# Neighbourhood attention items of two grid rows and four heads, scored in quarter products, with the bias loaded per item

## The chip, the cores and the metric

The kernel runs on one core of one Trainium2 chip. The metric is the device time of one execution in microseconds (us); the lower the better. The core has TensorE (PE: matmuls, whose weight loads are listed as PEld), VectorE (DVE), ScalarE (ACT), GpSimd (POOL) and the queue engine SyncE (SP), which issues most of the DMAs. Each engine runs its own instructions in order and waits for the others by semaphores.

## The reference, cut to what matters

Three transformer-like blocks over 1024 tokens of width 1024. The change touches only the first block's neighbourhood attention: 8 heads of 64 on a grid of 16 rows by 64 columns. A query of row r attends to 8 rows of keys, and there to 16 columns around its own; the kernel computes all 64 columns and masks the rest.

```python
def one_row(r):
    r0 = jnp.clip(r - kr // 2, 0, rows - kr)          # kr = 8, rows = 16
    k_band = lax.dynamic_slice_in_dim(kg, r0, kr, axis=1)[:, :, key_cols]
    v_band = lax.dynamic_slice_in_dim(vg, r0, kr, axis=1)[:, :, key_cols]
    q_row = lax.dynamic_index_in_dim(qg, r, axis=1, keepdims=False)
    s = jnp.einsum('bjqhd,brjkhd->bhjqrk', q_row, k_band).astype(jnp.float32) * scale
    dr = r0 + jnp.arange(kr) - r + NA_WIN_R - 1
    bias = jnp.take(rpb_cols, dr, axis=1)
    s = s + jnp.transpose(bias, (0, 2, 3, 1, 4))[None]
    s = jnp.where(mask, s, -jnp.inf)
    p = jax.nn.softmax(s.reshape(s.shape[:4] + (kr * NA_KSPAN_C,)), axis=-1).reshape(s.shape)
    o = jnp.einsum('bhjqrk,brjkhd->bjqhd', p.astype(v.dtype), v_band)
# afterwards: o_na = rms_norm(o_na, na_norm_g) per head, then the output projection
```

Beside it in the same block runs the gated delta rule (GDN): 4 heads of 128, two directions, 8 chunks of 128 tokens each, a chunk's result entering the next through a state S.

## The kernel before

The kernel is one hand-ordered program. The stage of interest ("the mixers") runs GDN and the neighbourhood attention at the same time. `gdn_slots()` gives 14 slots per chunk n; in each slot every engine first does its GDN piece, then its attention piece (`na_pe`, `na_act`, `na_dve`), then the piece of the GDN output norm (`gout_*`). A slot is no barrier: an engine goes on as far as its semaphores allow, but always in this order.

GDN per chunk: slot 0 puts out the previous chunk (`step_out`, state update), slots 1 to 12 build an inverse in six levels, each a ping-pong. PE multiplies ("Q", line 1334), DVE masks into `g_gu` (1512), PE multiplies again ("X", 1334), DVE subtracts into `g_Dc` (1521) and turns it into `g_D` (1500, 1503). Slot 13 is the V product (1323) and the next chunk's keys by keys (1267).

The attention walks over 16 items k, one grid row with all 8 heads each, seven slots apart. Its parts p of an item: p 0 to 3, one score product each (line 1622) for a pair of heads, and on DVE `biased` (1740) adds the bias and takes the row maximum in one instruction; p 4 and 5, ACT takes the exponential (1684), PE turns the result (1630), ACT copies it out (1692); p 7 and 8, PE weighs the values (1648); p 9 and 10, sum of squares and scaling `n_z` (1712 to 1771); p 11, PE multiplies `n_z` by a folded identity (1676) and ACT copies to the output (1729).

A score product is a full 128 by 128 array: the 64 dimensions of two heads on the contraction side, and as weights `n_zq`, which holds head 0's queries in its upper left quarter and head 1's in its lower right one, zeros elsewhere. The result is [2 heads x 64 queries, 512 keys], one PSUM bank. All operands are f32, for which the trace shows two passes per matmul. The bias of all shifts stays in SBUF as `n_bias`, [128, 4 x 15 x 64]. A grid row whose band of keys begins at an odd row (4 of 16) has a key order in two pieces, 448 and 64 columns.

PSUM has 8 banks: each GDN direction d has three, `gbank(d, i)` = 3d + i, and the attention has banks 6 and 7: scores and turned tiles in both, its outputs in 7.

## Time and profile before

| | us |
|---|---|
| median of 3 runs | 3765.86 (3764.18 to 3771.94) |
| the profiled execution | 3769.14 |
| its span from first to last instruction | 3767.4 |
| stage of the mixers in it, first score to last finish | 379.2 to 743.2 |
| PE, DVE, ACT, POOL busy over the span | 3702.6, 2153.1, 1580.1, 80.8 |

The mean granted clock is 0.996 of full speed. The busy time of an engine says how long it had an instruction in flight, not that it set the time; matmuls overlap, so their busy times and the durations of single ones are longer than their pitch. What a step costs PE in a stream is read from one start to the next. "Idle before" is the time the engine stood before a group, with what ended it.

### The profile page before, as it was taken

The page shows a single profiled execution, that of the slowest core. Times are in us where ns is not written, and L with a number is a line of the kernel's source. Part 1 is how long each engine was busy: PE and PEld are TensorE (multiplying, and loading weights), DVE is VectorE, ACT ScalarE, POOL GpSimd, SP SyncE. Part 2 cuts the span into 40 slices and gives each one's busy share as a digit, 9 for nine tenths or more (in the row PEclk, how much of TensorE's full clock was granted, in tenths as well). Part 3 has the DMA queues.
Part 4 walks back from the last instruction along what each step waited for, and adds up shares of the span by engine and source line. Part 5 has one row for each costly group of instructions (what it writes and reads, how often), then busy time and mean ns, then how long its engine had stood idle before and what let it go on. Part 6 is the DMA issues. An engine that isn't in the chain of part 4 may idle for free.

```text
span 3767.4 us, 50718 instructions
## 1 busy us (share of the span) xinstructions
PE 3702.6 (98%) x21185; PEld 2983.0 (79%) x21185; DVE 2153.1 (57%) x3300; ACT 1580.1 (42%) x2544; POOL 80.8 (2%) x85
## 2 busy tenths in 40 slices
PE   8999898899999999999999999999999999999998
PEld 5888677778888878888788889888787778788887
DVE  5641767776334668757588655266555266555333
ACT  5452566534333544435353442333433233434333
POOL 0000121000000000000000000000000000000000
PEclk9999999999999999999999999999999999999999
DMA  5122101233422222222222322222222222223222
GB/s 196 46 73 64 31 19 38 86 103 97 116 95 95 91 88 73 95 91 94 90 79 84 100 92 90 88 86 79 84 95 91 94 84 84 79 95 118 95 92 87
DMA packets 116363, 327.83 MB, mean 87 GB/s; under 512 B 27288, under 2 KB 34472, under 8 KB 116136
## 3 DMA queue, kind: packets, MB, share of 16 engines
q1 hardware_dynamic: 113896, 319.07, 25.6%
q0 software_dynamic: 2240, 5.51, 0.7%
q8 instruction: 169, 2.77, 0.3%
q14 instruction: 58, 0.48, 0.0%
HBM read 307.99 MB, written 18.09 MB: 87 GB/s over the span
## 4 chain that ended last, share of the span: by engine, by line
PE 95%; DVE 2%; ACT 1%; issue 1%; DMA 0%; SPq 0%; ACTq 0%; DVEq 0%
PE ps L329 54%; PE ps L307 28%; PE ps L1622 2%; PE ps L1323 2%; PE ps L807 1%; PE ps L1648 1%; PE ps L2785 1%; PE ps L1031 1%; PE ps L1334 1%; PE ps L1630 0%; DVE n_s L1740 0%; ACT n_s L1684 0%; PE ps L2220 0%; PE ps L2247 0%; PE ps L1364 0%
## 5 line engine op out<-in xcount | busy, mean ns | idle before, releaser
L329 PE MATMUL ps<-a,w_hi 128*128 128x512 f32 (+1 forms) x6064 | 1838.2, 388 | 3.8 <-issue 2.1
L329 PEld LDWEIGHTS ps<-a,w_hi 128*128 128x128 f32 x6064 | 1110.1, 188 | 262.0 <-issue 12.0
L329 PE MATMUL ps<-a,w_lo 128*128 128x512 f32 (+1 forms) x3032 | 1147.3, 385 | 0.0
L268 DVE TENSOR_TENSOR w_lo<-w_raw,w_hi 128x1024 fp32r<-128x1024 f32 x539 | 658.0, 1221 | 396.6 <-ACT w_hi L263 393.8
L263 ACT ACTIVATE w_hi<-w_raw 128x1024 fp32r<-128x1024 f32 x539 | 563.5, 1050 | 517.0 <-DMA w_raw<-in_w_mlp 323.8
L329 PEld LDWEIGHTS ps<-a,w_lo 128*128 128x128 f32 x3032 | 562.5, 188 | 119.7
L307 PE MATMUL ps<-h_hi,w_hi 128*128 128x512 f32 x1528 | 485.4, 399 | 0.0
L307 PE MATMUL ps<-h_hi,w_lo 128*128 128x512 f32 x1528 | 479.1, 395 | 0.0
L307 PE MATMUL ps<-h_lo,w_hi 128*128 128x512 f32 x1528 | 478.8, 395 | 0.0
L374 DVE TENSOR_TENSOR h_lo<-u_sq,h_hi 128x512 fp32r<-128x512 f32 x192 | 132.9, 692 | 461.5 <-ACT h_hi L364 460.7
L390 DVE TENSOR_TENSOR xT<-xT,ps 128x1024 f32<-128x1024 f32 x191 | 232.9, 1220 | 247.3 <-PE ps L307 246.4
L307 PEld LDWEIGHTS ps<-h_hi,w_lo 128*128 128x128 f32 x1528 | 288.1, 189 | 65.8
L307 PEld LDWEIGHTS ps<-h_lo,w_hi 128*128 128x128 f32 x1528 | 288.1, 189 | 65.5
L307 PEld LDWEIGHTS ps<-h_hi,w_hi 128*128 128x128 f32 x1528 | 284.9, 189 | 69.0 <-issue 4.4
L359 ACT ACTIVATE u_act<-ps 128x512 f32<-128x512 f32 x128 | 76.6, 598 | 346.2 <-PE ps L329 346.1
L2191 DVE SCALAR_TENSOR_TENSOR mixh<-c_pad,params,mixh 128x512 f32<-128x512 f32 x240 | 163.7, 744 | 0.0
L363 ACT ACTIVATE u_sq<-u_act 128x512 f32<-128x512 f32 x192 | 121.3, 632 | 18.3 <-ACT u_act L359 1.1
L359 ACT ACTIVATE u_act<-ps,params 128x512 f32<-128x512 f32 x64 | 44.1, 688 | 197.4 <-PE ps L329 197.4
L364 ACT ACTIVATE h_hi<-u_act 128x512 fp32r<-128x512 f32 x192 | 118.1, 615 | 0.0
L396 DVE TENSOR_TENSOR xT<-xT,ps 128x512 f32<-128x512 f32 x48 | 32.9, 686 | 133.9 <-PE ps L329 133.9
L2847 ACT ACTIVATE l_e<-l_e 128x256 f32<-128x256 f32 x56 | 23.4, 418 | 140.8 <-DVE l_e L2883 139.8
L1622 PE MATMUL ps<-n_k,n_zq 128*128 128x512 f32 (+2 forms) x160 | 73.9, 563 | 6.9 <-DVE n_small L1740 6.9
(394 smaller groups left out, 2971.8 us busy)
## 6 DMA issues: line engine op xcount, KB each, us to landing
...
w_raw<-in_w_in SPq DMA_DIRECT2D x107, 512.0 KB, 3.4
...
```

The costliest lines, as they stand in the source:

```text
L263: nc.scalar.activation(w_hi[u.z][:, :], w_raw[u.z][:, :], ACT.Copy).then_inc(w_hi_done[u.z], 1)
L268: nc.vector.tensor_tensor(w_lo[u.z][:, :], w_raw[u.z][:, :], w_hi[u.z][:, :].bitcast(F32), ALU.subtract).then_inc(w_split[u.z], 1)
L307: last = nc.tensor.matmul(ps[:, u.bank + c, :], w[:, k * 256 + c * P:k * 256 + (c + 1) * P], act[:, (u.first + k) % RING, :], start=(k == ...
L329: last = nc.tensor.matmul(ps[:, bank, 0:t1 - t0], w[:, k * P:(k + 1) * P], a[:, h, low, k, t0:t1], start=(i_k == 0 and i == 0), stop=(i_k ...
L359: nc.scalar.activation(u_act[:, s, :], ps[:, u.bank, :], ACT.Relu, bias=bias).then_inc(bank_free(u), 1)
L363: nc.scalar.activation(u_sq[:, s, :], u_act[:, s, :], ACT.Square)
L364: nc.scalar.activation(h_hi[:, u.chunk % RING, :], u_act[:, s, :], ACT.Square).then_inc(hid_hi, 1)
L374: nc.vector.tensor_tensor(h_lo[:, r, :], u_sq[:, u.chunk % 2, :], h_hi[:, r, :].bitcast(F32), ALU.subtract)\
L390: nc.vector.tensor_tensor(two, two, ps[:, u.bank:u.bank + 2, :], ALU.add).then_inc(bank_free(u), 1)
L1323: last = nc.tensor.matmul(pbank(b)[:, h, :], lhsT[:, h, :], rhs[:, h, :], start=start, stop=stop)
L1622: last = nc.tensor.matmul(ps[:, score_bank(k, c), t0:t1], n_zq[k % 2][:, c, :], n_k[:, c, row * GRID:row * GRID + t1 - t0], start=True, st ...
L2191: nc.vector.scalar_tensor_tensor(y, x, w, y, op0=ALU.mult, op1=ALU.add).then_inc(c_tap, 1)
```

## The change

An item is now one chunk of two grid rows (2c and 2c+1) with four of the eight heads; there are still 16 items. `item(k)` gives the chunk and the first pair of heads. A score call covers one pair of heads and both rows: four matmuls of 64 by 64 weights, one in each quarter of the array (contraction side: the head i; output side: the row j), which write the halves of banks 6 and 7. So the calls stand at p 0 and p 2 in place of p 0, 1, 2, 3. The queries `n_q` are loaded as they are, without zeros, with one DMA in place of two.

The bias differs between the two rows, so its slice per item is gathered: the masked table (now `n_tab`) is stored once to memory (`na_tab`), and `bias_item_sp` loads [128, 4, 512], 1 MB, into one of two buffers `n_bias`, whenever the slice differs from that two items before (10 items of 16). `biased` is then always one instruction of 512 columns; the second maximum of the odd rows is gone.

The attention's outputs go to bank 1 (even k) or 4 (odd k), which GDN also uses: so Q moves to bank 2 or 5, where X is, V to bank 0 or 3, and there are new waits: the GDN's output product of direction 1 and its k by q product wait for `n_z`, `weigh` waits for GDN's readers. The finish is two 128 by 128 transposes in place of eight 64 by 64 products; it waits for the next item's `biased`, since its bank 7 holds scores.

Cut diff (Q's, V's and the ACT and DVE lines that only follow the new banks and the renamed tiles are left out):

```diff
@@ -741,8 +741,9 @@
         g_bytok = xs.take("g_bytok", [2 * TC * GH, P])
         xs2 = Region(x_at, x_at + 4 * DC * T)
         n_k = xs2.take("n_k", [P, NP, T])
-        n_bias = xs2.take("n_bias", [P, NP, 2 * KR - 1, GRID])
-        n_mask = xs2.take("n_mask", [P, GRID])
+        n_tab = Region(xs2.at, xs2.stop).take("n_tab", [P, NP, 2 * KR - 1, GRID])
+        n_bias = [xs2.take(f"n_bias{i}", [P, NP, BAND]) for i in range(2)]
+        n_mask = main_tail.take("n_mask", [P, GRID])
 
         G_LOG, G_CUM, G_TOT, G_BETA, G_NEGDEC, G_KDEC, G_LAST, G_TMP = range(8)
         G_CUMB, G_NCUM = G_TOT, G_TMP
...
@@ -1356,6 +1357,9 @@
             def step_out(m, d):
                 pe.wait_ge(gs["vn"], last_once(m, d))
                 pe.wait_ge(gs["qd"], once(m, d))
+                pe.wait_ge(gs["qk"], once(m, d))
+                if d:
+                    pe.wait_ge(na["z"], 2 * m + 2)
                 for h in range(GH):
                     o = pbank(gbank(d, 1))[:, h, :]
 
...
@@ -1407,6 +1407,10 @@
                 if s == 8 and n >= 0:
                     for d in range(2):
                         c = toks(chunk_of(n, d))
+                        if n:
+                            pe.wait_ge(gs["oe"], once(m, d))
+                        if d == 0:
+                            pe.wait_ge(na["z"], 2 * n + 1)
                         heads(gbank(d, 1), g_kT[:, :, c], g_qT[:, :, c]).then_inc(gs["kq"], 1)
                 if s == 10 and n >= 0:
                     for d in range(2):
...
@@ -1591,36 +1598,51 @@
         def na_rows(i):
             return [(k, i - ROW_STEPS * k) for k in (i // ROW_STEPS - 1, i // ROW_STEPS) if 0 <= k < ROWS and i - ROW_STEPS * k <= 11]
 
-        def spans(k):
-
-            r0 = BANDS[k]
-            dr0 = r0 - RO[k] + KR - 1
+        def item(k):
+
+            return CHUNKS[k // 2], 2 * (k % 2)
+
+        def spans(r):
+
+            r0 = band(r)
+            dr0 = r0 - r + KR - 1
             if r0 % 2 == 0:
                 return [(0, BAND, r0, dr0)]
             return [(GRID, BAND, r0, dr0), (0, GRID, r0 + KR - 1, dr0 + KR - 1)]
 
-        def score_bank(k, c):
-
-            return 6 if k else 6 + c % 2
-
-        def out_heads():
-            return ps[:, 7, 0:NP * GRID].rearrange("p (c x) -> p c x", c=NP)
+        def item_bias(k):
+
+            return [(j, t0, t1, dr) for j in range(2) for t0, t1, _, dr in spans(2 * item(k)[0] + j)]
+
+        def new_bias(k):
+            return k < 2 or item_bias(k) != item_bias(k - 2)
+
+        def bias_loads(k):
+
+            return sum(2 * len(item_bias(i)) for i in range(k % 2, k + 1, 2) if new_bias(i))
+
+        def out_heads(k):
+            return ps[:, gbank(k % 2, 1), 0:NP * GRID].rearrange("p (t x) -> p t x", t=NP)
 
         def na_pe(pe):
-            def score(k, c):
-                if c == 0 and k:
-                    pe.wait_ge(na["ptc"], NP * k - 1)
-                if c == 0:
-                    pe.wait_ge(zq_in[k % 2], X_IN + 32 * (k // 2) + 32)
-                if k == 0 and c < 2:
-                    pe.wait_ge(nv_act, NV_LAST.index(6 + c) + 1)
-                elif k == 0:
-                    pe.wait_ge(na["m"], c - 1)
-                elif c:
-                    pe.wait_ge(na["m"], NP * k + c)
-                for t0, t1, row, _ in spans(k):
-                    last = nc.tensor.matmul(ps[:, score_bank(k, c), t0:t1], n_zq[k % 2][:, c, :], n_k[:, c, row * GRID:row * GRID + t1 - t0], start=True, stop=True)
-                last.then_inc(na["s"], 1)
+            def score(k, pair):
+                c, first = item(k)
+                if pair == 0:
+                    pe.wait_ge(zq_in[k % 2], X_IN + 16 * (k // 2) + 16)
+                    if k:
+                        pe.wait_ge(na["ptc"], NP * k)
+                    else:
+                        pe.wait_ge(nv_act, TC)
+                else:
+                    pe.wait_ge(na["m"], NP * k + 2)
+                pieces = [(j, t0, t1, row) for j in range(2) for t0, t1, row, _ in spans(2 * c + j)]
+                for j, t0, t1, row in pieces:
+                    for i in range(2):
+                        part = slice(GRID * i, GRID * i + GRID)
+                        last = nc.tensor.matmul(ps[GRID * j:GRID * j + GRID, 6 + i, t0:t1], n_q[k % 2][part, pair, GRID * j:GRID * j + GRID],
+                                                n_k[part, first + pair, row * GRID:row * GRID + t1 - t0], start=True, stop=True)
+                        if (j, t0, t1, row) == pieces[-1]:
+                            last.then_inc(na["s"], 1)
 
             def turn(k, c):
                 pe.wait_ge(na["p"], NP * k + c + 1)
@@ -1630,30 +1652,33 @@
                     last = nc.tensor.transpose(ps[:, 6 + c % 2, t * P:(t + 1) * P], n_s[:, c, t * P:(t + 1) * P], const("ident"))
                 last.then_inc(na["pt"], 1)
 
-            def weigh(k, c):
-                r0 = BANDS[k]
+            def weigh(k, t):
+                c, first = item(k)
+                head = (first + t // 2) * P + t % 2 * GRID
                 pe.wait_ge(na["ptc"], NP * k + NP)
-                for t in range(KR // 2):
-                    if r0 % 2 == 0:
-                        v = n_v[:, r0 // 2 + t, c * P:(c + 1) * P]
-                    elif t == 0:
-                        i = ODD.index(k)
-                        pe.wait_ge(vx_in[i % 2], X_IN + 32 * (i // 2) + 32)
-                        v = n_vx[i % 2][:, c * P:(c + 1) * P]
-                    else:
-                        v = n_v[:, (r0 + 1) // 2 + t - 1, c * P:(c + 1) * P]
-
+                if k % 2:
+                    pe.wait_ge(gs["qk"], once(k // 2, 1))
+                elif k:
+                    pe.wait_ge(gs["oe"], once(k // 2 - 1, 0))
+                for b in range(KR // 2):
                     for j in range(2):
+                        r0 = band(2 * c + j)
+                        if r0 % 2 == 0:
+                            v = n_v[:, r0 // 2 + b, head:head + GRID]
+                        elif b == 0:
+                            i = ODD.index(k // 2)
+                            pe.wait_ge(vx_in[i % 2], X_IN + 32 * (i // 2) + 32)
+                            v = n_vx[i % 2][:, head:head + GRID]
+                        else:
+                            v = n_v[:, (r0 + 1) // 2 + b - 1, head:head + GRID]
                         part = slice(GRID * j, GRID * j + GRID)
-                        last = nc.tensor.matmul(ps[part, 7, c * GRID:(c + 1) * GRID], n_pt[c][:, t, part], v[:, part], start=(t == 0),
-                                                stop=(t == KR // 2 - 1))
+                        last = nc.tensor.matmul(out_heads(k)[part, t, :], n_pt[t][:, b, part], v, start=(b == 0), stop=(b == KR // 2 - 1))
                 last.then_inc(na["av"], 1)
 
-            pe.wait_ge(nb_done, 1)
             for i in range(GDN_STEPS):
                 for k, p in na_rows(i):
-                    if p < 4:
-                        score(k, p)
+                    if p in (0, 2):
+                        score(k, p // 2)
                     if p == 5:
                         normed = i - EARLY + 6 - OUT_FIRST - 8
                         if normed >= 0:
@@ -1670,11 +1695,11 @@
                         weigh(k, 2 * (p - 7) + 1)
                     if p == 11:
                         pe.wait_ge(na["z"], k + 1)
-                        for c in range(NP):
-                            for j in range(2):
-                                part = slice(GRID * j, GRID * j + GRID)
-                                last = nc.tensor.matmul(ps[part, 7, c * GRID:(c + 1) * GRID], n_z[part, c, :], const("fold")[part, :],
-                                                        start=True, stop=True)
+                        if k + 1 < ROWS:
+                            pe.wait_ge(na["m"], NP * (k + 1) + NP)
+                        for i in range(2):
+                            last = nc.tensor.transpose(ps[:, 7, i * P:(i + 1) * P], n_z[:, 2 * i:2 * i + 2, :].rearrange("p t x -> p (t x)"),
+                                                       const("ident"))
                         last.then_inc(na["f"], 1)
                 yield
...
         def na_dve(dve):
-            def biased(k, c):
-                dve.wait_ge(na["s"], NP * k + c + 1)
+            def biased(k, t):
+                dve.wait_ge(na["s"], NP * k + t + 1)
+                if t == 0:
+                    dve.wait_ge(bias_in[k % 2], 16 * bias_loads(k))
                 if k:
-                    dve.wait_ge(na["pt"], NP * (k - 1) + c + 1)
-                for j, (t0, t1, _, dr) in enumerate(spans(k)):
-                    bias = n_bias[:, c, dr:dr + (t1 - t0) // GRID, :].rearrange("p r x -> p (r x)")
-                    ins = nc.vector.tensor_tensor_reduce(n_s[:, c, t0:t1], ps[:, score_bank(k, c), t0:t1], bias, 1.0, -3.0e38, op0=ALU.add, op1=ALU.max,
-                                                         accum_out=n_small[:, N_MAX + j, c:c + 1])
-                ins.then_inc(na["m"], 1)
+                    dve.wait_ge(na["pt"], NP * (k - 1) + t + 1)
+                nc.vector.tensor_tensor_reduce(n_s[:, t, :], ps[:, 6 + t % 2, :], n_bias[k % 2][:, t, :], 1.0, -3.0e38, op0=ALU.add, op1=ALU.max,
+                                               accum_out=n_small[:, N_MAX, t:t + 1]).then_inc(na["m"], 1)
...
         def queries_sp(sp, k):
+            c, first = item(k)
             if k >= 2:
                 sp.wait_ge(na["s"], NP * (k - 1))
-            for j in range(2):
-                part = slice(GRID * j, GRID * j + GRID)
-                sp.dma_start(n_zq[k % 2][part, :, part], g["nq1"][:, part, GRID * RO[k]:GRID * RO[k] + GRID].rearrange("c p t -> p c t"))\
-                    .then_inc(zq_in[k % 2], 16)
+            sp.dma_start(n_q[k % 2][:, :, :], g["nq1"][first:first + 2, :, toks(c)].rearrange("c p t -> p c t")).then_inc(zq_in[k % 2], 16)
+
+        def bias_item_sp(sp, k):
+            c, first = item(k)
+            if k >= 2:
+                sp.wait_ge(na["m"], NP * (k - 1))
+            for j, t0, t1, dr in item_bias(k):
+                for i in range(2):
+                    src = g["na_tab"][GRID * i:GRID * i + GRID, first:first + 2, dr:dr + (t1 - t0) // GRID, :].rearrange("p c r x -> p c (r x)")
+                    sp.dma_start(n_bias[k % 2][GRID * j:GRID * j + GRID, i:NP:2, t0:t1], src).then_inc(bias_in[k % 2], 16)
...
         def mixers_sp(sp):
-            sp.wait_ge(n_zero, 1)
+            sp.wait_ge(stored, 16 * 2 * GH)
             queries_sp(sp, 0)
             queries_sp(sp, 1)
+            sp.wait_ge(nb_done, 1)
+            sp.dma_start(g["na_tab"], n_tab[:, :, :, :]).then_inc(stored, 16)
+            sp.wait_ge(stored, 16 * 2 * GH + 16)
+            bias_item_sp(sp, 0)
+            bias_item_sp(sp, 1)
             sp.wait_ge(nv_act, TC)
             odd_v_sp(sp, 0)
             odd_v_sp(sp, 1)
```

The order on PE in the middle of the fourth chunk (slots 3 to 6): the two weigh calls, the score calls and between them Q and X, of which each is sixteen small matmuls. Before, one 128-row score after every step:

```order
L1648 MATMUL ps<-n_v,n_pt_135 64x64 x8
L1622 MATMUL ps<-n_k,n_zq_83 128x512
L1334 MATMUL ps<-g_gu_108,g_D_110 64x8x4
...
L1648 MATMUL ps<-n_v,n_pt_137 64x64 x8
L1622 MATMUL ps<-n_k,n_zq_83 128x512
L1334 MATMUL ps<-g_Dc_112,g_A_114 64x4x8
...
L1622 MATMUL ps<-n_k,n_zq_83 128x512
L1334 MATMUL ps<-g_gu_108,g_D_110 64x4x8
```

Now, in the same stretch:

```order
L1675 MATMUL ps<-n_v,n_pt_137 64x64 x8
L1642 MATMUL ps<-n_k,n_q_83 64x512 x4
L1335 MATMUL ps<-g_gu_110,g_D_112 64x8x4
...
L1675 MATMUL ps<-n_v,n_pt_139 64x64 x8
L1335 MATMUL ps<-g_Dc_114,g_A_116 64x4x8
...
L1642 MATMUL ps<-n_k,n_q_83 64x512 x4
L1335 MATMUL ps<-g_gu_110,g_D_112 64x4x8
```

Four full products per item have become two groups of four quarter products; the one between the second weigh pair and Q is gone, and the one behind the next X too.

The order on SP ahead of the mixers and in the first chunk. Before, queries (`n_zq`), shifted values (`n_vx`) and decay rows (`g_row`):

```order
L1956 DMA n_zq_82<-nq 64x4x64 x2
L1956 DMA n_zq_83<-nq 64x4x64 x2
L1965 DMA n_vx_139<-n_v 64x512 x2
L1965 DMA n_vx_140<-n_v 64x512 x2
L1925 DMA g_row_141<-gate_rows 128x512
```

Now:

```order
L1971 DMA n_q_82<-nq 128x2x128
L1971 DMA n_q_83<-nq 128x2x128
L1995 DMA na_tab<-n_tab 128x3840
L1980 DMA n_bias_106<-na_tab 64x2x512 x4
L1980 DMA n_bias_107<-na_tab 64x2x512 x4
L1988 DMA n_vx_141<-n_v 64x512 x2
L1988 DMA n_vx_142<-n_v 64x512 x2
L1945 DMA g_row_143<-gate_rows 128x512
```

The store of the table and eight loads of it stand ahead of the values and the decay rows.

## Rows read from the trace of the kernel before

**Rows 1.** Page, part 1: busy time, share of the span, instructions of each engine.
```profile
PE 3702.6 (98%) x21185; PEld 2983.0 (79%) x21185; DVE 2153.1 (57%) x3300; ACT 1580.1 (42%) x2544; POOL 80.8 (2%) x85
```

**Rows 2.** Windows, one per chunk: length, busy us per engine, clock, DMA.
```profile
423.00:466.00 43.00, 39.51 (x683) 31.54 (x682) 32.75 (x105) 28.17 (x83) 7.43 (x6) 1.00 0.09 26
510.50:555.00 44.50, 40.99 (x682) 32.32 (x681) 30.95 (x100) 26.27 (x77) 7.43 (x6) 0.96 0.07 20
648.00:698.00 50.00, 44.24 (x687) 35.30 (x686) 35.21 (x111) 28.93 (x81) 7.87 (x6) 0.93 0.10 27
```

**Rows 3.** Chain of waits, 381 to 743 us, shares by line.
```profile
by line: PE ps L1622 16.5%; PE ps L1323 16.4%; PE ps L1648 10.3%; PE ps L1334 6.9%; issue 5.1%; PE ps L1630 4.9%; DVE n_s L1740 4.9%; ACT n_s L1684 4.9%; PE ps L1364 3.9%; PE ps L1363 3.5%; PE ps L1267 3.5%; DVE g_D L1503 2.9%; PE ps L1353
```

**Rows 4.** Line 1622, the scores: ns min/median/max, forms, who waits.
```profile
L1622 PE MATMUL ps<-n_k,n_zq x160: 219/592/1220, 379.2 to 719.4; 128*128 128x512 f32 x96, 128*128 128x448 f32 x32, 128*128 128x64 f32 x32
...
  DVE n_small L1740: 17.8, 49
...
  DVE n_s L1740: 53.7, 40
```

**Rows 5.** Timeline of PE from 519.3 us: start, us, what, [idle before].
```profile
520.35 1.15 PE L1648 MATMUL ps<-n_v,n_pt 128*64 128x64 f32 x32
521.43 1.13 PE L1622 MATMUL ps<-n_k,n_zq 128*128 128x512 f32 x2
522.49 0.67 PE L1334 MATMUL ps<-g_gu,g_D 64*64 64x32 f32 x32
523.09 1.15 PE L1648 MATMUL ps<-n_v,n_pt 128*64 128x64 f32 x32
```

**Rows 6.** Timeline of PE, 544 to 546 us.
```profile
544.04 0.68 PE L1346 MATMUL ps<-g_Dc,g_A 64*64 64x64 f32 x16
544.65 1.15 PE L1648 MATMUL ps<-n_v,n_pt 128*64 128x64 f32 x32
```

**Rows 7.** Timeline of PE, 1443.2 to 1446 us (block 2 scores).
```profile
1443.38 2.00 PE L2247 MATMUL ps<-s_k,s_q 64*128 64x256 f32 x16
1445.31 0.72 PE L329 MATMUL ps<-a,w_hi 128*128 128x512 f32 x2
```

**Rows 8.** Line 1740, biased: ns min/median/max, forms.
```profile
L1740 DVE CUSTOM_DVE_ANT_0 n_s<-ps,n_bias x80: 219/682/693, 381.1 to 720.3; 128x512 f32<-128x512 f32 x48, 128x448 f32<-128x448 f32 x16, 128x64 f32<-128x64 f32 x16
```

**Rows 9.** Timeline of DVE, 515 to 532 us.
```profile
522.60 0.69 DVE L1740 CUSTOM_DVE_ANT_0 n_s<-ps,n_bias 128x512 f32<-128x512 f32 x1 [1.29 <-PE ps L1622]
...
525.33 0.69 DVE L1740 CUSTOM_DVE_ANT_0 n_s<-ps,n_bias 128x512 f32<-128x512 f32 x1 [0.61 <-PE ps L1622]
...
527.35 0.49 DVE L1512 TENSOR_TENSOR g_gu<-ps,g_lev 128x128 f32<-128x128 f32 x2
...
531.25 0.69 DVE L1740 CUSTOM_DVE_ANT_0 n_s<-ps,n_bias 128x512 f32<-128x512 f32 x1 [1.24 <-PE ps L1622]
```

**Rows 10.** Timeline of PE, 525 to 533 us.
```profile
528.09 0.67 PE L1334 MATMUL ps<-g_gu,g_D 64*64 64x32 f32 x32 [0.88 <-DVE g_gu L1512]
529.14 2.07 PE L1622 MATMUL ps<-n_k,n_zq 128*128 128x512 f32 x2 [0.38 <-DVE n_small L1740]
```

**Rows 11.** Timeline of ACT, 543.9 to 549.9 us.
```profile
547.06 2.45 ACT L1299 ACTIVATE g_dec<-g_dec,g_gates 128x128 f32<-128x128 f32 x8
549.42 0.36 ACT L1712 ACTIVATE n_zsq<-ps 128x256 f32<-128x256 f32 x1
```

**Rows 12.** Queries' DMAs on SP, line 1956: ns min/median/max, first and last start.
```profile
L1956 SPq DMA_DIRECT2D n_zq<-nq x32: 573/610/1513, 332.0 to 671.6; - x32
```

**Rows 13.** DMA, 299 to 316 us: issues, KB each, us to landing.
```profile
n_bias<-rpb_rows SPq DMA_DIRECT2D x8, 240.0 KB, 5.7
```

**Rows 14.** Windows: around a fall of the clock, and ahead of the stage.
```profile
525.70:529.10 3.40, 1.99 (x49) 0.97 (x42) 3.29 (x13) 0.50 (x2) 0.00 (x0) 1.00 0.00 0
529.10:532.50 3.40, 3.36 (x10) 2.33 (x10) 2.09 (x8) 0.00 (x0) 0.00 (x0) 0.50 0.02 5
346.00:379.00 33.00, 33.00 (x153) 27.02 (x152) 4.32 (x10) 4.80 (x9) 0.00 (x0) 1.00 0.00 0
```

71 lines of the change are left out of this document (31 added, 40 removed).

## Prediction

> **What bounds the kernel now.** I read the page first, then the windows by chunk, the chain of waits, the score line and the timelines of one chunk. PE is busy 98% of the span [rows 1], but the stage of the mixers (379 to 743 us) is looser: a chunk takes 43.0 us with PE busy 39.51, DVE 32.75 and ACT 28.17, a later one 44.5, and those in which the GDN output norm joins 50.0 [rows 2]. So PE is nearly the bound, with a small idle part in which DVE and ACT set the pace. In the chain of waits over the stage the score line 1622 is the largest piece, 16.5% of 362 us, which is 60 us [rows 3]; nearly every score product lies on the path. Around them DVE waits 53.7 us in total for scores, and PE 17.8 us for DVE's reading of the last one [rows 4].
>
> **The change part by part.**
>
> *The scores on PE, removed.* 16 items times 4 products. A product is two passes and takes 521.43 to 522.49 = 1.06 us [rows 5]. That is 64 x 1.06 = 67.8 us (the 16 in two pieces, 448 and 64 columns, taken as the same).
>
> *The scores on PE, added.* 16 items times 2 groups of four quarter products, each of two passes of 512 columns. Nothing in the trace has four quarters with 512 columns; three rows bound it. Four quarters at once: Q and X are 16 quarter products of 32 columns, 32 passes in 522.49 to 523.09 = 0.60 us, 19 ns each [rows 5]. Line 1346 uses two quarters at a time: 16 passes in 544.04 to 544.65 = 0.61 us, 38 ns each [rows 6]. Twice the quarters, half the time per pass: four quarters do work side by side, at least where loading weights is what takes the time. Two halves of the contraction side with a longer stream: 16 passes of 256 columns in 1443.38 to 1445.31 = 1.93 us, so 0.24 us per pair of passes [rows 7], while 512 columns on the whole array take 0.53 a pass: the two halves overlap fully. Line 1648, two halves of the output side, takes 32 passes in 1.08 us, 34 ns each, less than the 38 of the quarters. So I take a group as two passes of 512 columns, twice 0.24 to 0.48 for twice the columns each: 0.9 us plus the start, 0.93. The bounds: 0.93 if all four overlap; 1.8 if two at a time do; about 3.7 if none does. I take 0.93, since all rows with less than the whole array show overlap. Sum 32 x 0.93 = 29.8 us; the eight odd items add two short pieces per group, about 0.12 us each, 2 us. PE loses 67.8 - 31.8 = 36 us of work.
>
> By the Trainium skill, TensorEngine Tiling (Array Packing), section Restrictions and Gotchas, different row tiles cannot use one PSUM bank at the same time. In Q and X both row halves write into one bank, and they take 19 ns a pass all the same [rows 5], so the trace doesn't bear it out as a serialization; here the two heads write banks 6 and 7 anyway. Were the rule to bite somewhere, the result would be the second rival's.
>
> *The finish.* Eight quarter products with 16 passes, at 38 ns [rows 6] 0.6 us, become two transposes with 4 passes; a 128-column pass is about a quarter of the 0.53 of a 512-column one, so 0.13, 0.5 in all. 0.1 x 16 = 1.6 us at most; I count it in the chunk below.
>
> *DVE.* The four odd rows lose 16 extra instructions of 64 columns, at 0.22 us (the least of the line) to 0.69 [rows 8], and four small ones: 4 to 10 us over the stage, none in the early chunks, and half of it in cover. Its four waits on scores per item become one: after the first `biased` of a pair, the second finds its bank full.
>
> *The walk through one chunk.* The fourth chunk runs from 504.02 to 548.62, 44.6 us. At 521.43 the first score starts on both kernels. Before, DVE runs `biased` at 522.60 after 1.29 us of idling and the second at 525.33 after 0.61 [rows 9]; that one holds up its turns and `g_gu` at 527.35, and so PE, which waits 0.88 for X at 528.09 [rows 9, 10]. After, the second `biased` runs without a wait, and X comes at about 527.3, 0.8 earlier: less than the 2.1 us of scores cut on PE, since DVE is now the slower one. Then the 2.07 us of the last score goes (at half clock, [rows 10]) and with it DVE's wait of 1.24 [rows 9]; DVE's own work (scaling, turns, `g_gu`) puts the next X at 531.9 in place of 534.8, 2.9 earlier. Behind slot 8 the same pattern comes again for the next item, with two products of 1.06 ahead of the V product: about 4.6 earlier there. At the chunk's end ACT's exponentials (2.45) stand ahead of the squares at 549.42 [rows 11], and DVE's chain behind the squares takes a us of the gain away and gives it back as PE no longer puts a score between keys by keys and `step_out`. I get 39 to 39.5 us for the chunk at full clock, and allow 0.7 for the clock (below) and the new waits: 40.0, a gain of 4.6. PE then has 41.0 - 8.5 + 3.7 - 0.2 = 36.0 us of work in 40.0 [rows 2], DVE 31: tight but possible.
>
> *New waits.* `step_out` of direction 1 waits for `n_z` of the odd item, behind it the state update, the finish and the next Q. In the walk both come within 0.4 us of each other; it can cost 0 to 0.5 a chunk, and it is in the 0.7. The k by q product waits for `n_z` of slot 6, two slots past. The finish waits for the next item's last `biased`, which has no wait of its own any more. V in bank 0 or 3 waits for `kd`, three slots past. These cost nothing in that walk, and up to 0.3 each if DVE slips.
>
> *The table.* Storing 1.97 MB and loading two items of 1 MB go behind the masked table and to where the first load of queries stands, 332.0 [rows 12]. Eight DMAs of 240 KB landed at 5.7 us each, all between 300 and 316 [rows 13]: 1.9 MB in some 15 us. So the store ends by 347 and the loads by 363; from 346 to 379 the DMA engines are empty, [rows 14], and the first `biased` is at 381. Cover: 17 us. Later loads are 1 MB, some 8 us, issued about 20 us ahead of use on an SP queue that otherwise waits. Nothing on the path. The first score waits for the last copy of the values, about 0.8 us later, and gives it back but for 0.2.
>
> *The sum.* Chunk 0: 4.0; chunks 1 to 3: 3 x 4.6 = 13.8; chunks 4 to 6, longer by pieces of the output norm that ACT and DVE pace: 3 x 4.0 = 12.0; chunk 7, with only one item to score: 2.3; less 0.2 at the start. 31.9 us. What follows the stage is PE-bound and moves as a whole. The profiled execution was 3769.1 us, so 3737; against the median, 3765.9 - 32 = 3734.
>
> **The clock.** Right before a fall the engine was busy 1.99 of 3.40 us; then it had the lower of its two levels, 1.2 in place of 2.4 GHz, for 3.4 us [rows 14]. The mean clock is 0.96 in most chunks, one such fall each, 0.93 in a later one [rows 2]. The change thins out PE's work exactly there (slots 5 and 6), so falls will not get rarer. By the Trainium skill, TensorE: Matmul & The Clock Gate, section on the two states, the engine runs at half rate unless kept busy, which is what the row shows; it speaks against a change that takes PE's densest work away.
>
> **The rivals.**
> *Half the gain is eaten by DVE and ACT* (0.12): PE falls idle and the ping-pong sets the chunk. For it: the first X gains only 0.8 of 2.1. Against it: DVE is busy 31 of 44.5. If the gain per chunk is 2.3: 18 us, 3748.
> *Quarters overlap only in pairs at 512 columns* (0.09): a group takes 1.8; PE saves 67.8 - 57.6 - 2 = 8 us, with the finish 10: 3756. For it: the passes of 32 columns are so short that weight loading may hide it [rows 5]. Against it: the two contraction halves overlap in full at 256 columns [rows 7], and nothing shows all four.
> *The clock, slower than before* (0.05): a chunk has 34.5 us of PE work at full clock (39.5 - 8.5 + 3.7 - 0.2) and some 3.5 of idling. With a share f of the time at half clock it is 34.5 / (1 - f/2) + 3.5; it passes 44.6 once f is over 0.32, against 0.08 now. At f = 0.5 a chunk takes 49.5, 5 more, +35 us: 3800.
> *It does not do what it says* (0.04): the bias arrives late or a new wait holds each chunk for 4 us, so that the gain is gone: 3762 to 3770.
> The forecast has 0.70.
>
> **How the numbers follow.** Faster (by over 0.2%, 7.5 us, about what a measurement of this kernel can tell from none): 0.70 + 0.12 + 0.09 = 0.91. Same 0.03, slower 0.06, from the last two. The range: low end, all of PE's saving plus four us of half-clock scores, 3766 - 44 = 3722; high end, the pairwise rival, 3757.
>
> **What would show it.** Right: a score group of 8 passes that takes about 0.93 us up to the next start; the score line under 8% of the stage's chain; DVE's waits for scores under 25 us; chunks of 39 to 41 us; PE waiting on `g_gu` more than before; n_bias loads with no one waiting. Wrong: groups of 1.8 us; a PEclk under 0.85 in the chunks; PE waiting for `n_z` ahead of `step_out` by over 1 us; the stage starting later than 380 us.

## The result, and the profile after

The changed kernel takes 3742.36 us (median of four runs, 3740.22 to 3745.01). The kernel before took 3766.53 beside it (3764.18 to 3771.94). The ratio is 0.9934, with a 95% interval of 0.9917 to 0.9951, so 24 us are gained where 32 were forecast; 3742 lies inside the range of 3722 to 3757. The profiled execution spans 3740.3 us in place of 3767.4, at a mean clock of 0.994.

In the lines of the changed kernel 1622 has become 1642 (scores), 1740 is 1764 (bias and maximum), 1648 is 1675 (value products), 1630 is 1652 (turns), 1334 is 1335 (Q and X), 1323 is 1324, 1684 is 1709 (exponents), 1692 is 1717 (turned copies).

The page after, against [rows 1], busy time of each engine:

```profile
PE 3668.1 (98%) x21121; PEld 2968.0 (79%) x21121; DVE 2148.3 (57%) x3262; ACT 1580.2 (42%) x2544; POOL 81.5 (2%) x85
```

PE lost 34.5 us of busy time; 36 were forecast, and up to 1.6 for the finish. DVE lost 4.8, where 4 to 10 were forecast.

Windows of three chunks, against [rows 2] (length, busy us of PE, PEld, DVE, ACT, POOL, clock, DMA):

```profile
497.40:537.00 39.60, 34.93 (x680) 29.69 (x676) 30.66 (x99) 26.48 (x77) 7.45 (x6) 1.00 0.32 76
578.40:620.90 42.50, 37.32 (x690) 31.38 (x686) 32.00 (x102) 28.04 (x80) 7.46 (x6) 0.96 0.16 46
666.20:709.60 43.40, 36.26 (x670) 31.15 (x665) 32.14 (x101) 29.68 (x82) 2.51 (x2) 0.96 0.11 30
```

A chunk with the clock full throughout takes 39.6 us, PE busy 34.9 in it and DVE 30.7.

The score group on PE, against [rows 5]:

```profile
512.73 1.15 PE L1675 MATMUL ps<-n_v,n_pt 128*64 128x64 f32 x32
513.81 1.09 PE L1642 MATMUL ps<-n_k,n_q 64*64 64x512 f32 x8
514.72 0.62 PE L1335 MATMUL ps<-g_gu,g_D 64*64 64x32 f32 x32
```

From 513.81 to 514.72 are 0.91 us for four quarter products of 512 columns, less than one product of the whole array took before (1.06). The four overlap in full. The groups of the items with an odd band, 12 passes with the short pieces among them, take the same 0.91 (the 0.12 that I added for them does not appear):

```profile
532.66 1.10 PE L1642 MATMUL ps<-n_k,n_q 64*64 64x512 f32 x12
533.57 0.63 PE L1347 MATMUL ps<-g_Dc,g_A 64*64 64x64 f32 x16
```

The chain of waits over 378 to 720 us, against [rows 3]:

```profile
by line: PE ps L1324 13.3%; issue 8.4%; PE ps L1675 7.7%; PE ps L1642 7.0%; DVE n_s L1764 5.8%; PE ps L1335 5.7%; DVE g_D L1508 5.2%; ACT n_s L1709 3.9%; PE ps L1652 3.6%; PE ps L1367 3.5%; DVE g_gu L1517 3.2%; PE ps L1368 3.1%; PE ps L1354
```

Scores went from 16.5% of it to 7.0%, and VectorE's lines came up. What the score line waits for (`n_small`) and who waits for it (`n_s`), against [rows 4] (us, times):

```profile
L1642 PE MATMUL ps<-n_k,n_q x320: 216/589/1112, 379.7 to 689.1; 64*64 64x512 f32 x96, 64*64 64x448 f32 x32, 64*64 64x64 f32 x32
...
  DVE n_small L1764: 13.9, 16
...
  DVE n_s L1764: 32.9, 15
```

Timeline of VectorE over the same stretch as the walk's, against [rows 9]:

```profile
514.95 0.69 DVE L1764 CUSTOM_DVE_ANT_0 n_s<-ps,n_bias 128x512 f32<-128x512 f32 x1 [1.26 <-PE ps L1642]
...
517.00 0.68 DVE L1764 CUSTOM_DVE_ANT_0 n_s<-ps,n_bias 128x512 f32<-128x512 f32 x1
...
519.00 0.49 DVE L1517 TENSOR_TENSOR g_gu<-ps,g_lev 128x128 f32<-128x128 f32 x2
...
520.04 0.69 DVE L1764 CUSTOM_DVE_ANT_0 n_s<-ps,n_bias 128x512 f32<-128x512 f32 x1
```

From 514.95 VectorE has no gap until 525.7: the first bias waits 1.26 us for its scores, and all behind it goes through without a wait. The chain in this stretch, 512.7 to 523 us, is now VectorE's but for the two PE groups ahead of it:

```profile
by line: DVE n_s L1764 23.9%; DVE g_D L1508 12.8%; PE ps L1675 11.2%; PE ps L1642 10.6%; issue 10.5%; DVE g_S L1535 8.3%; DVE g_D L1505 7.7%; DVE g_Dc L1526 6.3%; DVE g_gu L1517 4.7%; DVE n_small L1781 3.3%; DVE n_small L1764 1.1%; DVE n_sm
```

Before, the same stretch (520.35 to 530.6 us of the kernel before) was PE's:

```profile
by line: PE ps L1622 41.0%; PE ps L1648 21.8%; DVE n_s L1740 13.5%; DVE g_D L1503 8.6%; PE ps L1334 5.8%; DVE g_gu L1512 4.8%; DVE g_D L1500 3.5%; DVE n_small L1761 3.3%; issue 2.9%; DVE n_small L1759 0.7%; DVE n_small L1763 0.3%; DVE n_sma
```

The bias is loaded from the table with nobody waiting, at a median of 4.7 us for each of 36 loads (against [rows 13]):

```profile
n_bias<-na_tab SPq DMA_DIRECT2D x36, 256.0 KB, 4.7
```

The stage measured by the start of each V product (`g_R` by `g_Dt`), which ends a chunk:

| | V of chunk 0 | steps to the V of chunks 1 to 7 | last finish |
|---|---|---|---|
| before | 418.2 | 41.2, 44.6, 44.6, 44.9, 47.5, 50.9, 45.0 | 742.9 |
| after | 418.6 | 38.9, 39.9, 39.6, 41.4, 42.5, 45.3, 43.4 | 717.3 |
| gain | -0.4 | 2.3, 4.7, 5.0, 3.5, 5.0, 5.6, 1.6 | 25.6 in all |

Between the last V and the last finish 1.7 us are lost again. So the early and last pieces fall short, the middle ones are as forecast. Of the 0.4 us lost up to the V of chunk 0, 0.5 lie ahead of the first score (379.69 for 379.20); from there the chunk takes 38.95 us, before 39.02. At the start the changed kernel runs with a low clock. PE, and the window behind it:

```profile
379.69 1.09 PE L1642 MATMUL ps<-n_k,n_q 64*64 64x512 f32 x8 [0.78 <-ACT n_v L826]
382.19 1.09 PE L1642 MATMUL ps<-n_k,n_q 64*64 64x512 f32 x8 [1.41 <-DVE n_small L1764]
...
385.75 1.97 PE L1652 MATMUL ps<-consts,n_s 128*128 128x128 f32 x8 [2.03 <-ACT n_s L1709]
```

```profile
385.00:395.00 10.00, 9.25 (x120) 7.36 (x124) 3.83 (x13) 7.30 (x20) 4.97 (x4) 0.51 0.58 146
```

Three idle stretches of 0.8, 1.4 and 2.0 us, then 10.2 us at the lower of the two levels (granted 0.51), and 6.8 more from 402 on. The kernel before idled 0.6 and 1.2 us there, and 0.7 later, and ran at full clock until 403. The trace's clock records add up to 37.4 us at the lower level in the stage, and 23.8 before.

### The profile page after: what moved, and what is told of

The parts are those of the page before. It is cut to its first block, busy times and chain, and to the rows that moved or that the text cites. A ratio compares the mean times of both kernels' runs of the same rounds, so it can differ in the third digit from the quotient of the medians.

```text
span 3740.3 us, 50657 instructions
## 1 busy us (share of the span) xinstructions
PE 3668.1 (98%) x21121; PEld 2968.0 (79%) x21121; DVE 2148.3 (57%) x3262; ACT 1580.2 (42%) x2544; POOL 81.5 (2%) x85
## 4 chain that ended last, share of the span: by engine, by line
PE 94%; DVE 3%; ACT 2%; issue 1%; DMA 0%; SPq 0%; ACTq 0%; DVEq 0%
PE ps L329 54%; PE ps L307 28%; PE ps L1324 1%; PE ps L808 1%; PE ps L2815 1%; PE ps L1032 1%; PE ps L1675 1%; PE ps L1642 1%; DVE n_s L1764 1%; PE ps L1335 1%; DVE g_D L1508 0%; PE ps L2250 0%; PE ps L2277 0%; ACT n_s L1709 0%; PE ps L2239 0%
## 5 line engine op out<-in xcount | busy, mean ns | idle before, releaser
L329 PEld LDWEIGHTS ps<-a,w_hi 128*128 128x128 f32 x6064 | 1110.0, 188 | 260.5 <-issue 10.6
L363 ACT ACTIVATE u_sq<-u_act 128x512 f32<-128x512 f32 x192 | 121.3, 632 | 18.3 <-ACT u_act L359 1.1
L464 ACT ACTIVATE a<-mixh 128x512 fp32r<-128x512 f32 x64 | 40.5, 633 | 78.8 <-DVE mixh L498 77.6
```

The costliest lines, as they stand in the source:

```text
L329: last = nc.tensor.matmul(ps[:, bank, 0:t1 - t0], w[:, k * P:(k + 1) * P], a[:, h, low, k, t0:t1], start=(i_k == 0 and i == 0), stop=(i_k ...
L363: nc.scalar.activation(u_sq[:, s, :], u_act[:, s, :], ACT.Square)
L464: nc.scalar.activation(a[:, m.half, 0, c, META:W], src, ACT.Copy).then_inc(m.s["hi"], 1)
```

## The experiments

All times are medians; each kernel ran beside the kernel before, which took 3766.1 to 3768.0 us. "More" and "less" are against the 3742.36 of the changed kernel, unless another kernel is named.

### What a microsecond on each engine costs

**Every score group twice**

```diff
-                for j, t0, t1, row in pieces:
+                for again in range(2):
+                    for j, t0, t1, row in pieces:
...
-                        if (j, t0, t1, row) == pieces[-1]:
+                            if again and (j, t0, t1, row) == pieces[-1]:
```

> The changed kernel with every group of quarter products issued twice (the same result into the same banks, the second one is waited for). It adds 32 groups of 0.91 us = 29 us of PE work. Theory A (PE is still what mostly sets the chunk, and what was cut from it came back nearly whole): 22 to 29 us more than the changed kernel, about 3768. Theory B (after the change DVE and ACT set the ping-pong, and PE idles): 5 to 14 us more, about 3752. If the lower clock is what ate part of the gain, the denser PE shows fewer stretches at half clock than the 37 us of the changed kernel.

3758.26 us (3752.76 to 3762.02), ratio 0.9973 (0.9964 to 0.9982): 15.9 more, of 28.8 us that PE was given (65.3 busy on the line in place of 36.5). So 55% comes through, between the two theories (5 to 14 and 22 to 29 us). PE is no longer the full bound, but its work still counts. The stage is at the lower clock level for 27.2 us in place of 37.4, less, as expected of a denser PE.

**An additional copy on ScalarE ahead of each turned copy** (the copy is used by nothing)

```diff
+                act.wait_ge(na["ptc"], NP * k + c)
+                nc.scalar.activation(n_scr[:, :], ps[:, 6 + c % 2, :], ACT.Copy)
                 nc.scalar.activation(n_pt[c][:, :, :].rearrange("p t x -> p (t x)"), ps[:, 6 + c % 2, :], ACT.Copy).then_inc(na["ptc"], 1)
```

> The changed kernel with one more ACT copy of 512 columns (to a tile nobody reads) ahead of each of the 64 copies of turned tiles: 64 x 0.5 = 32 us of ACT work, each between the turns on PE and the weighing. Theory A (PE): under 12 us more. Theory B with ACT as the one that sets the chunk: 25 us or more. With DVE as the one: under 12 us.

```profile
L1719 ACT ACTIVATE n_scr<-ps 128x512 f32<-128x512 f32 x64 | 38.0, 594 | 12.5 <-PE ps L1653 7.1
```

3768.07 us (3765.46 to 3769.38), ratio 1.0002 (0.9993 to 1.0012): 25.7 more of 38.0 added, 68%; theory B with ScalarE had 25 or more. The lower level took 64.7 us of the stage in place of 37.4, so that a part of this is the clock's. ScalarE, busy 64% of the stage, has no room where it counts: the exponents, the turns and the turned copies follow one another.

**An additional copy on VectorE ahead of each bias**

```diff
+                if NP * k + t:
+                    dve.wait_ge(na["m"], NP * k + t)
+                nc.vector.tensor_copy(n_scr[:, :], ps[:, 6 + t % 2, :])
                 nc.vector.tensor_tensor_reduce(n_s[:, t, :], ps[:, 6 + t % 2, :], n_bias[k % 2][:, t, :], 1.0, -3.0e38, op0=ALU.add, op1=ALU.max,
```

> Ahead of each of the 64 bias-and-maximum instructions VectorE copies the same 512 scores from the bank to a scratch tile (some 0.6 us each, 38 us in all; the copy is used by nothing). Theory A (PE is the bound, VectorE and ScalarE have room between the score groups): half or less comes through, under 19 us, 3745 to 3761 us. Rival B (the first score group, the bias of tiles 0 and 1 and the second group follow one another with PE idle, and the exponents wait for the last bias): nearly all of it comes through, 30 us or more, 3772 us or above.

```profile
L1767 DVE COPY n_scr<-ps 128x512 f32<-128x512 f32 x64 | 43.7, 683 | 34.1 <-PE ps L1643 33.5
```

3778.05 us (3772.11 to 3781.16), ratio 1.0025 (1.0015 to 1.0034): 35.7 more of 43.7 added, 82%. The rival's case. Not all of it is VectorE's own: with PE waiting more, the lower clock level took 81.7 us of the stage in place of 37.4. In chunk 1, which has no such stretch, 3.8 us came of 5.5 added, 70%.

The three prices, 55, 68 and 82%, sum to far more than one: a chain goes to and fro between the engines, and each of them is on it for a part of a chunk. Their order, however, does not rank the engines, since the clock differs between the runs. Chunks with the same clock in both kernels give 67% for PE (chunk 3, no low stretch: 42.0 us for 39.6, of 3.6 added), 70% for VectorE (chunk 1 above) and 89% for ScalarE (chunk 2, 3.4 us at the lower level in each: 44.1 for 39.9, of 4.75 added), from one execution each. As an estimate, the cut at the prices of the medians, 34.5 x 0.55 + 4.8 x 0.82 = 23 us, is close to the 24 gained.

### The overlap of the quarters

**Quarter by quarter, each piece cut in two**

```diff
-                for j, t0, t1, row in pieces:
-                    for i in range(2):
+                for j in range(2):
+                    for i in range(2):
+                        for t0, t1, row, _ in spans(2 * c + j):
+                            half = (t0 + t1) // 2
+                            for u0, u1 in ((t0, half), (half, t1)):
...
```

> Each score group is issued quarter by quarter, the pieces of a quarter one behind another and each cut in two (16 products a group where there were 4 or more), so that neighbours in the queue mostly need the same quarter of the array. Theory A (the four quarters run side by side only because neighbours in the queue belong to different quarters): a group grows from 0.91 us to between 2 and 3.7 us (one quarter alone is 512 columns at two passes, some 1.1 us), PE gets 30 to 90 us more of busy time, and by the 15 to 19 us that came through of 29 in the doubled score groups the time goes to 3760 to 3790 us. Rival B (the array sorts it out, whatever the order): the group stays below 1.2 us and the time within 4 us of the changed kernel.

PE's timeline of a group of an even band and of one of an odd band:

```profile
514.62 1.11 PE L1644 MATMUL ps<-n_k,n_q 64*64 64x256 f32 x16
515.53 0.64 PE L1335 MATMUL ps<-g_gu,g_D 64*64 64x32 f32 x32
...
535.35 1.84 PE L1644 MATMUL ps<-n_k,n_q 64*64 64x256 f32 x21
537.01 0.27 PE L1347 MATMUL ps<-g_Dc,g_A 64*64 64x64 f32 x2
```

3748.65 us (3747.73 to 3750.12), ratio 0.9948 (0.9934 to 0.9963): 6.3 more. Neither theory holds as written. With four passes of a quarter in a row (even bands, 16 passes) the group still takes 0.91: the array does sort it out. In an item with an odd band one of the two rows has two pieces, so that its quarters get eight passes in a row and the other row's four (24 passes in all). This group takes 1.66 to 2.0, where the changed kernel's 12 passes over the same columns, quarter after quarter in turn, take 0.91. In the group at 535.35 the trace has the first passes of three quarters at 535.35 to 535.38 and that of the fourth, which stands in the queue behind the eight of the third, only at 536.19. Its passes are then all that is in flight:

```profile
L1644 PE MATMUL ps<-n_k,n_q 64*64 64x224 f32 x3 | 0.7, 349 | 0.0
```

(PE's lines by form, 536.7 to 537.0 us.) The number of passes alone is hardly the reason, since 32 of Q or X go in 0.60 us [rows 5]. Sixteen such groups times 0.75 or more are 12 us of PE work and 6.3 us of time, half, as in the doubled groups. So the way in which the products are written carries a part of the gain, and a group as long as the pairwise rival's 1.8 does occur, for another order and another cut. The late fourth quarter speaks for the order; no run has the order without the cut.

### The clock

**Products that nothing uses in the start's idle stretches**

```diff
                     else:
+                        pe.wait_ge(nv_act, 2)
+                        filler(256)
                         pe.wait_ge(nv_act, TC)
                 else:
+                    if k == 0:
+                        filler(512)
+                        filler(128)
                     pe.wait_ge(na["m"], NP * k + 2)
...
+                if k == 0 and c == 0:
+                    filler(512)
+                    filler(256)
+                    filler(128)
```

> The changed kernel with six products that nobody reads, put into bank 0 in the gaps where PE waits at the start of the stage (before the first score group, before the second, before the first turn; 0.5, 1.3 and 1.8 us). Theory C (the first chunk lost its gain because PE stood still 4.2 us of 6, and its clock then was at half for 10.2 and 6.8 us): the clock holds over 385 to 409 us, the first V product comes at about 414.5 in place of 418.6, and the end 4 us earlier, 3738. Rival (the start is late for the wait on the values' last copy and the ACT chain): no change in the first V product, or later by the fillers, within 1 us.

The first 26 us of the stage, with the fillers and without:

```profile
378.00:404.00 26.00, 20.57 (x396) 14.45 (x395) 17.26 (x58) 13.11 (x35) 7.48 (x6) 0.90 0.54 129
```

```profile
378.00:404.00 26.00, 18.02 (x342) 12.49 (x341) 16.73 (x56) 11.71 (x31) 7.47 (x6) 0.77 0.39 98
```

The clock is 0.90 in place of 0.77, and the V product of chunk 0 starts at 415.2 in place of 418.6. The median, 3740.63 (3737.82 to 3741.83), ratio 0.9927 (0.991 to 0.9943), is 1.7 us lower, within the intervals. Counted from the first score, chunk 0 takes 35.9 us in place of 38.95, with 6.8 us at the lower level in place of 17.0. In this execution, then, the low clock cost chunk 0 most of its gain; whether it does so in the median is taken up with the last pair.

**The same, and fillers in every chunk**

```diff
+                    if k % 2:
+                        pe.wait_ge(gs["S"], once(k // 2, 0))
+                        filler(256)
...
+                if s == 6 and n >= 0:
+                    nc.tensor.matmul(ps[:, 0, 0:256], all_ones, n_k[:, 0, 0:256], start=True, stop=True)
```

> The start's fillers as in the run before, and in each of the eight chunks two more idle stretches filled with a product of 256 columns that nothing uses: ahead of the second score group of the odd item and ahead of the third level's second products. Theory A (the half-clock stretches that remain, some 27 us of them in the stage, each begin behind an idle stretch of PE and cost about half of their length): they go for the most part, and the stage gains up to 10 us on the start's fillers alone, 3731 to 3737 us. Rival B (the fillers delay the chain by as much as the clock returns, or the falls begin elsewhere): within 3 us of the kernel with the start's fillers, 3738 to 3744 us, or above it.

3738.24 us (3735.65 to 3739.59), ratio 0.9918 (0.9902 to 0.9935): 2.4 below the run before, 20.4 us at the lower level in place of 27.2. This is the rival's case (within 3 us); another 2 us are within what the intervals leave open.

### Where the wait sits

**The second score group a slot later** (with the start's fillers, as all kernels below but the last)

```diff
-                    if p in (0, 2):
-                        score(k, p // 2)
+                    if p in (0, 3):
+                        score(k, p // 3)
...
-                    if p < 4:
+                    if p < 2:
                         biased(k, p)
+                    if p == 3:
+                        biased(k, 2)
+                        biased(k, 3)
```

> The start's fillers as before, and the second score group of each item one slot later, behind the level products of the two heads (slot 3 in place of 2, with both of its bias instructions in slot 3). Theory A (PE stands idle for the bias of tile 1 in slot 2 of each item, 7 us in the stage, and that is on the path): the stage gains 3 to 7 us, 3733 to 3738 us. Rival B (the exponents then wait, since the last bias comes later by one PE pass; ScalarE's chain from exponent to turned copy was found on the path): no gain or a loss, 3741 to 3755 us.

```profile
L1776 DVE CUSTOM_DVE_ANT_0 n_s<-ps,n_bias 128x512 f32<-128x512 f32 x64 | 42.7, 688 | 38.7 <-PE ps L1650 38.5
L1650 PE MATMUL ps<-n_k,n_q 64*64 64x512 f32 (+2 forms) x320 | 40.4, 595 | 0.4 <-ACT n_v L826 0.3
```

3758.94 us (3752.94 to 3768.02), ratio 0.9979 (0.9969 to 0.9989). PE's wait for the bias is gone to nearly nothing (0.3 us), and 18.3 us are lost against the kernel with the start's fillers, more than rival B allowed (3755). VectorE now waits 38.5 us for scores in place of 31.4, but most of the loss is the clock's: chunk 1, with the clock full, takes 39.8 us, only 0.8 more than with the fillers alone, and chunk 2, with 10.2 us at the lower level, 4.5 more:

```profile
455.40:499.50 44.10, 38.86 (x669) 32.24 (x669) 31.00 (x100) 26.48 (x77) 7.44 (x6) 0.88 0.28 68
```

68.0 us of the stage are at the lower level in place of 27.2. The work is the same (DVE 31.0, ACT 26.5 in the chunk). What has changed is that PE idles once for 2.7 us ahead of X, where it idled 0.7, 0.9 and 1.1 us apart from each other. In chunks 2 to 5 the clock fell for 10.2 us at this stretch, in chunk 1 it did not:

```profile
438.18 0.67 PE L1335 MATMUL ps<-g_gu,g_D 64*64 64x32 f32 x32 [2.67 <-DVE g_gu L1517]
...
478.81 1.08 PE L1335 MATMUL ps<-g_gu,g_D 64*64 64x32 f32 x32 [2.73 <-DVE g_gu L1517]
```

So one long idle stretch makes a fall likely, not certain. This is the mechanism of the clock rival, and its price was about right: its formula gives 4.5 us more for 10.2 us of a 44.1 us chunk at half clock; 4.5 were measured, of which some 0.8 came with full clock too.

**The value products of tiles 0 and 1 a slot later, so that the next item's first scores stand ahead of them**

```diff
-                    if p in (7, 8):
-                        weigh(k, 2 * (p - 7))
-                        weigh(k, 2 * (p - 7) + 1)
+                    if p == 8:
+                        for t in range(NP):
+                            weigh(k, t)
```

> The start's fillers as before, and the value products of an item's tiles 0 and 1 move one slot later, so that the first score group of the next item stands directly behind the level products of slot 3 or 10 and in front of the next level products. Theory A (VectorE is the engine that has no room, all that was added to it came through, and it waits 32.9 us in 15 waits for score groups that stand behind value products of 1.1 us): the waits fall by 1 us each, the steps of the chunks by 1 to 2 us each, 3724 to 3732 us. Rival B (VectorE then waits for the next thing, since the level products themselves come no earlier): within 3 us of the kernel with the start's fillers, 3738 to 3744 us.

```profile
L1776 DVE CUSTOM_DVE_ANT_0 n_s<-ps,n_bias 128x512 f32<-128x512 f32 x64 | 43.9, 688 | 16.3 <-PE ps L1650 15.8
```

3726.31 us (3724.36 to 3727.47), ratio 0.989 (0.9875 to 0.9905): 14.3 less than with the start's fillers alone, as theory A had it (3724 to 3732). VectorE's wait for scores fell from 31.4 us in that kernel to 15.8, 15.6 us, and nearly all of it came through, with no engine given less work. A part may be the clock's, since 20.4 us of the stage are at the lower level in place of 27.2. Of the single moves tried, this is the wait that pays most.

**Exponents ahead of the last output copy on ScalarE**

```diff
-                for k, p in na_rows(i):
+                for k, p in reversed(na_rows(i)):
```

> The start's fillers as before; ScalarE does the first two exponents of an item ahead of the output copy of the item before, for whose transposes it waits 1.9 and 2.8 us in a chunk. Theory A (ScalarE's chain from exponent to turned copy is on the path, as 26 us of 32 that came through there say): PE's waits for n_s and n_pt (10 us in the stage) fall by half or more and 0.5 to 1.5 us a chunk is gained, 3730 to 3737 us. Rival B (VectorE sets the pace there and PE only waits elsewhere): within 3 us of the kernel with the start's fillers, 3738 to 3744 us.

```profile
L1664 PE MATMUL ps<-consts,n_s 128*128 128x128 f32 x256 | 35.1, 280 | 3.4 <-ACT n_pt L1729 2.6 <-ACT g_vt L1839 0.4 <-ACT n_s L1721 0.3
```

3734.32 us (3733.18 to 3735.64), ratio 0.9912 (0.9897 to 0.9927): 6.3 less than with the start's fillers alone. PE's idle time ahead of the turns is 3.4 us, where it was 11.5 in that kernel (12.4 in the changed one).

**Both, and the squares a slot earlier**

```diff
-                    if p == 9:
+                    if p == 8:
                         act.wait_ge(na["av"], NP * k + NP)
```

> Both edits of the two kernels beside it and a third: the squares for the output norm one slot earlier on ScalarE, ahead of the exponents of slot 12, behind which VectorE waits 2.2 us for them in a chunk. Theory A (all three waits are on the path that runs through VectorE): 2.5 to 4 us a chunk, 3712 to 3724 us. Rival B (the waits share one cover, so that only one of them pays): no better than the better of the two kernels beside it by more than 2 us.

3723.82 us (3723.27 to 3726.13), ratio 0.9885 (0.9869 to 0.9902): 2.5 below the better of the two. The steps of chunks 1 to 4 are 37.8 to 38.1, but 14.3 + 6.3 do not add up: theory A's 3712 to 3724 is met only at its edge, and what it rests on (each wait pays for itself) is not.

**Two moves on VectorE besides**

```diff
-                if s in (2, 4) and 0 < n < TC:
-                    d = s // 2 - 1
+                if s in (1, 3) and 0 < n < TC:
+                    d = s // 2
...
-                if s == 8 and n >= 0:
+                if s == 9 and n >= 0:
                     for d in range(2):
                         dve.wait_ge(gs["kq"], once(n, d))
```

> The three edits and the start's fillers as in the run before, and on VectorE two more moves: the state updates of slots 2 and 4 stand in slots 1 and 3 behind the masked products, where VectorE waits 1.0 and 0.4 us for the level products, and the masking of g_qk stands in slot 9 in place of 8, where it waits 0.6 and 0.2 us for PE. Theory A (VectorE sets the pace of a chunk and each of its waits is on the path): up to 2 us a chunk for seven chunks, 3711 to 3720 us. Rival B (PE waits already for the masked products, and the moved work delays the level results by as much as it saves): within 3 us of the kernel with the three edits, 3721 to 3727 us.

Waits of VectorE ahead of the level results, in the kernel with three edits and with five:

```profile
L1526 DVE TENSOR_TENSOR g_Dc<-g_Dc,ps 128x128 f32<-128x128 f32 x80 | 19.2, 281 | 10.7 <-PE ps L1335 10.6
```

```profile
L1526 DVE TENSOR_TENSOR g_Dc<-g_Dc,ps 128x128 f32<-128x128 f32 x80 | 19.1, 280 | 2.7 <-PE ps L1335 2.5
```

3714.09 us (3711.93 to 3715.73), ratio 0.9862 (0.9848 to 0.9877): 9.7 less than with three edits. The waits went from 10.6 to 2.5 us and, at `g_qk`, from 8.1 to none, since work that does not need the level results now stands where VectorE waited for them; its waits for scores fell too, from 14.3 to 7.4. Of these 23 us less than half came through as time.

**The five moves without fillers**

> The five moves without the start's fillers. Theory A (the half-clock stretch at the start is the same whatever follows, and the fillers gave 1.7 us by the medians and 2.5 us by the spans): 1 to 4 us above the kernel beside it. Rival B (the fillers' gain was a draw of where the clock fell): within 1 us of it.

3711.81 us (3710.44 to 3713.46), ratio 0.9858 (0.9842 to 0.9874). It is 2.3 us faster than with the fillers, where theory A had 1 to 4 more and rival B the same within 1, so neither is met, though the spreads of the two kernels overlap. No gain of the fillers is shown. PE idles 0.78, 1.41 and 2.03 us at the start as in the changed kernel, and this time the clock fell at 384 for 6.8 us and at 401 for 3.4, in place of 10.2 and 6.8; the V product of chunk 0 starts at 414.3. From the first score it takes 35.3 us, as with the fillers (35.4), where the changed kernel took 38.95. The same idle stretches are followed by low stretches of different length. This version beats both kernels: 54.3 us less than before, 30.6 less than the changed one. A chunk at full clock:

```profile
450.70:487.30 36.60, 33.81 (x670) 28.99 (x668) 30.36 (x100) 26.31 (x78) 7.45 (x6) 1.00 0.35 81
```

PE is busy 33.8 of 36.6 us there.

## Why the prediction was right, and where it was off

*The score group.* Right: 0.91 for 0.93. (The working's own rows give twice 0.48, or 0.96; the 0.93 was rounded down on the way, 1 us over 32 groups.) The choice between the bounds of 0.93, 1.8 and 3.7 decided the forecast, and the quarter-by-quarter run shows that a group near the middle bound can be had: 1.66 to 2.0 for odd bands, at 6.3 us for half of the groups.

*The walk through a chunk.* Right: 39 to 39.5 us were forecast at full clock, 39.6 measured; 40.0 with the clock, and the steps of chunks 1 to 3 are 38.9 to 39.9. VectorE as the next bound after the first bias is what the chain shows.

*Chunk 1.* Off by the baseline. I took the 44.6 us of the third step for all three early chunks; but the first took 41.2 in the trace of before. It had no fall of the clock, which half of a 3.4 us stretch, 1.7 us, can explain; the rest stays open. The gain there was 2.3 where 4.6 were in the sum.

*Chunk 0.* The term that failed: 4.0 forecast, 0.1 measured from the first score on, and the start 0.5 late for 0.2. The walk's pattern was carried to a chunk whose start is different: PE has nothing beside the scores to do, so that shorter scores turn into idle time (0.6 and 1.2 us became 1.4 and 2.0), and 17.0 us at the lower clock level followed where 3.4 had been. From the first score on, the chunk takes 3.0 us less with fillers and 3.6 less in the last kernel's execution without them (the five moves themselves did little there: 35.4 with fillers, for 35.9). So 3 to 3.6 of the 4.0 are there when the low stretch is shorter. The forecast had said that falls would not get rarer, and put 0.7 a chunk on it, but nothing on the start. How often the long low stretch comes was not settled; two pairs of medians disagree on the fillers' sign (1.7 less, 2.3 more).

*Chunks 4 to 6 and 7.* 14.1 measured for 12.0; 1.6 for 2.3. *Behind the last V* 1.7 are lost, which the sum did not have. The largest new wait there is the one on `n_z` ahead of `step_out`:

```profile
713.59 0.46 PE L1367 MATMUL ps<-g_qd,g_S 128*128 128x128 f32 x2 [1.99 <-DVE n_z L1791]
```

I had named it at 0 to 0.5 a chunk. In `step_out` it takes 3.5 us in four waits in the stage and 2.0 of them here, where no other work of PE stands between. That it accounts for the 1.7 is read from this row; no run took it away.

*The sum.* Gains at the V products 27.3, less 1.7: 25.6, against 31.9 forecast. Chunk 0 with the start is 4.2 of the difference (3.8 were forecast for the two), chunk 1 2.3, the last chunk 0.7, the end 1.7; chunks 2 to 6 give 2.6 back. By the spans the whole program gains 27.1, by the medians 24.2; the 1.5 behind the stage and the rest lie within the runs' spread.

*The rivals.* The pairwise overlap did not come, and the clock as a loss came in experiments alone (the copies on ScalarE and VectorE, the later score group), not in the change. By the total alone, the rival in which VectorE and ScalarE eat half of the gain did better than my forecast: 3742.4 lies 6 us below its 3748 and 8 above my 3734. But it is not the rival's mechanism, which was a gain of 2.3 us a chunk: chunks 2 to 6 gained 3.5 to 5.6, and what is missing is at the two ends and in chunk 1's baseline. One of its marks did go its way. VectorE's waits for scores are 32.9 us where I wanted under 25, because the first score group of an item still stands behind a value product, and its 15 waits hold VectorE 2.2 us each. The run that moved the value product shows this as the largest thing left, 14.3 us. The waits for `g_gu` grew as forecast, from 14.0 to 18.9 us.

*By the marks of the forecast.* Met: score line 7.0% of the chain for under 8; start of the stage 379.7 for under 380; bias loads with no one waiting; clock over 0.85 in chunks 1 to 7 (0.92 to 1.00). Two signs of being wrong came all the same, and name the pieces that fell short: the clock in chunk 0, 0.77 in its first 26 us, and PE's wait for `n_z` ahead of `step_out`, 2.0 us once where over 1 was the sign.
